# Hybrid encoder layer on one core: the first transfers of the SP queue in another order, and two waits and four small operations moved later

## The chip, the core and the metric

The kernel runs on one core of a Trainium2 chip. The metric is device time in microseconds of one execution. Each engine (TensorE, VectorE, ScalarE, GpSimd) works through its own list of instructions in order and waits on semaphores; SyncE (SP) issues nearly all DMA transfers from one list, in the order in which they are written.

## The reference, cut to what matters

Two inputs, 256 and 512 tokens of 1024 features, go through one encoder layer. Cut to its start:

```
def encoder_layer(x, norm1, w_in, ...):
    u = rmsnorm(x, norm1)
    z = u @ w_in                      # 1024 -> 384 + 256 + 32 + 512 + 512 columns
    q_lat, kv_lat, k_rope, x_br, g_br = jnp.split(z, [c1, c2, c3, c4], axis=-1)
    att = mla(q_lat, kv_lat, k_rope, q_norm, w_q_up, kv_norm, w_kv_up)
    lru = rglru_mixer(x_br, g_br, conv_w, conv_b, w_rg, b_rg, w_ig, b_ig, lru_lambda)
    ...
def rglru_direction(x, w_r, b_r, w_i, b_i, lam, reverse):
    ...
    log_a = -LRU_C * r * jax.nn.softplus(-lam.astype(jnp.float32))
```

Behind it come the output projection with the residual, a second norm, a mixture of 32 experts of which each token takes two, and a final norm.

## The kernel before

The 768 tokens are six x tiles of 128 rows. The change lies in the first 45 us, in the input stage. For each x tile, ScalarE squares and sums the row (`row_norm`, L1041) and takes the root with eps from the constants (L1045); VectorE takes the reciprocal (L1503) and writes x times rstd times the norm row (L1506, tile `un`); TensorE turns the tile with eight transposes against the identity in the constants (L660); ScalarE writes a rounded copy `u_high` (`input_high`, L1051) and VectorE the rest `u_low` (`input_low`, L1514). The columns of `w_in` come in 14 tiles of 1024 x 128 (the one for the rotary key is narrower): of each, ScalarE (the first four, `weight_high`, L1057) or GpSimd writes `w_high`, and GpSimd writes `w_low` (L535). TensorE multiplies in three passes, high by high, low by high, high by low, 24 matmuls to a unit (L716). Units 0 to 3 are the first four w_in tiles on the 256 tokens of the first input (x tiles 0 and 1); from unit 4 on come units of 512 columns too, which need all six x tiles. TensorE's order is: turn x tiles 0 and 1; unit 0; turn x tile 2; unit 1; turn tile 3; unit 2; turn tile 4; unit 3; turn tile 5; unit 4 and on. ScalarE moves finished units from PSUM to SBUF (`move_out`, L1079); the first goes into `xb`, which GpSimd clears at the start (semaphore `pads`, L524).

`cols` holds gains, biases and the decay parameters lambda by partition, `consts` the identity, eps and tables, `norm_row` the first norm's gain in all partitions. VectorE begins with four small operations on `cols` (L1496 to L1499) that prepare the decay constants; they are needed only behind the input stage.

The order is written out by hand for every engine. In SP's list a load of w_in tile t waits, from t = 2 on, until `w_low` of tile t - 2 is written (L366), and what stands behind it waits too.

Of the kernel before, what the change touches and what calls it, by code (L numbers as in the profile page):

```python
# [4 lines left out]
P = 128  # L5
TOK, PROMPT = 768, 256
NT = TOK // P
D = 1024
# [27 lines left out]
COLS = {}  # L36
# [16 lines left out]
def encoder_layer(nc, A_x, A_cols, A_consts, A_rope, A_rows, A_win, A_wq, A_wkv, A_wrg, A_wig, A_wout,  # L53
                  A_wrt, A_wgate, A_wup, A_wdown, y_prompt, y_sample):
    f32, f32r, i32 = mybir.dt.float32, mybir.dt.float32r, mybir.dt.int32
    ALU = mybir.AluOpType
# [3 lines left out]
    with ctx:  # L60
        def sb(name, shape, dt=f32):
            return ctx.enter_context(nc.sbuf_tensor(name, shape, dt))
# [32 lines left out]
        consts = sb("consts", [P, NCONSTS])  # L95
        cols = sb("cols", [P, NCOLS])
        norm_row = sb("norm_row", [P, D])
# [29 lines left out]
        def col(name, j, p0=0, p1=P):  # L127
            a = COLS[name] + j
            return cols[p0:p1, a:a + 1]
# [47 lines left out]
        lam_t = small[:, 32:80].rearrange("p (k n) -> p k n", k=6)  # L177
        hb_r = small[:, 80:88]
        hb_i = small[:, 88:96]
# [100 lines left out]
        def g(name):  # L280
            return S[name]
# [10 lines left out]
        def width(kind):  # L292
            return RP if kind == "k" else P
# [57 lines left out]
        def _(sp):  # L351
            xv = A_x.rearrange("(i p) d -> i p d", p=P)

            def load_x(i):
                if i == 5:
                    sp.wait_ge(g("un"), 1)
                sp.dma_start(xin[i], xv[i]).then_inc(s_xin[i], 16)
            wv = A_win.rearrange("(c p) n -> p c n", p=P)

            def load_w(t):  # L360

                kind, c = w_tiles[t]
                if t >= 2:
                    sp.wait_ge(g("wlo"), t - 1)
                col0, m = first_col[kind] + c * P, width(kind)
                sp.dma_start(w_raw[:, t % 2, :, 0:m], wv[:, :, col0:col0 + m]).then_inc(g(f"wr{t % 2}"), 16)  # L366
            load_x(0)
            sp.dma_start(cols[:], A_cols).then_inc(g("cols"), 16)
            sp.dma_start(consts[:], A_consts).then_inc(g("consts"), 16)
            sp.dma_start(norm_row[:], A_rows[3:4, 0:D].to_broadcast([P, D])).then_inc(g("n1"), 16)  # L370
            load_w(0)
            load_x(1)
            load_w(1)
            load_x(2)
            load_w(2)
            load_x(3)
            load_w(3)
# [650 lines left out]
        def _(ac):  # L1028
            chain = [0]

            def link(ins):
                chain[0] += 1
                ins.then_inc(g("ach"), 1)
                ac.wait_ge(g("ach"), chain[0])
# [4 lines left out]
            def row_norm(i):  # L1039
                ac.wait_ge(s_xin[i], 16)  # L1040
                link(ac.activation(junk, xin[i], ACT.Square, accum_out=ssq[:, i:i + 1]))  # L1041
                if i == 0:
                    ac.wait_ge(g("consts"), 16)
                    ac.wait_ge(g("cols"), 16)
                ac.activation(rstd1[:, i:i + 1], ssq[:, i:i + 1], ACT.Sqrt, bias=eps, scale=1.0 / D).then_inc(g("sd"), 1)  # L1045

            def input_high(i):

                for j in range(2):
                    ac.wait_ge(g("uTp"), 2 * i + j + 1)  # L1050
                    ac.activation(uh[:, 4 * j:4 * j + 4, i * P:(i + 1) * P],  # L1051
                                  psum[4 + 2 * (i % 2) + j][:, :].rearrange("p (c t) -> p c t", c=4),
                                  ACT.Copy).then_inc(g("uTh"), 1)

            def weight_high(t):
                ac.wait_ge(g(f"wr{t % 2}"), 16 * (t // 2 + 1))
                ac.activation(wh[:, t, :, :], w_raw[:, t % 2, :, :], ACT.Copy).then_inc(g("whi"), 1)  # L1057

            def move_out(u):

                kind, c, n = units[u]
                ac.wait_ge(g("zp"), u + 1)
                t0, tn = CHUNKS[n]
                if kind == "x":
                    dst = xb[:, c, XOFF[n] + 1:XOFF[n] + 1 + tn]
                elif kind == "z":
                    dst = zl[:, c, t0:t0 + tn]
                elif kind == "k":
                    dst = kr[0:RP, t0:t0 + tn]
                else:  # L1070
                    dst = gg[:, c, t0:t0 + tn]
                if kind == "z":
                    ins = ac.activation(sqz[:, c, t0:t0 + tn], psum[u % ZB][:, 0:tn], ACT.Square)
                    if n == 1:
                        ins.then_inc(g("sqz"), 1)
                    gain = col("q_norm", c) if c < QC else col("kv_norm", c - QC)
                    ac.activation(dst, psum[u % ZB][:, 0:tn], ACT.Copy, scale=gain).then_inc(g("ze"), 1)
                else:
                    ac.activation(dst, psum[u % ZB][0:width(kind), 0:tn], ACT.Copy).then_inc(g("ze"), 1)  # L1079

            ac.wait_ge(g("pads"), 1)
            row_norm(0)
            row_norm(1)
            weight_high(0)
            input_high(0)
            input_high(1)
            weight_high(1)
            row_norm(2)
            for i in range(2, NT):
                if i + 1 < NT:  # L1090
                    row_norm(i + 1)
                input_high(i)
                if i < W_RING:
                    weight_high(i)
                move_out(i - 2)

            ac.wait_ge(g("lam"), 1)
# [386 lines left out]
        def _(v):  # L1484
            chain = [0]

            def link(ins):
                chain[0] += 1
                ins.then_inc(g("dch"), 1)
                v.wait_ge(g("dch"), chain[0])  # L1490
            v.memset(ahead, 1.0).then_inc(g("ahead"), 1)
            v.wait_ge(g("cols"), 16)


            lam = cols[:, COLS["lam"]:COLS["lam"] + 8]
            link(v.tensor_scalar(lam_t[:, 4, :], lam, -1.0, None, ALU.mult))  # L1496
            link(v.tensor_tensor(lam_t[:, 0, :], lam_t[:, 4, :], lam, ALU.max))
            link(v.tensor_scalar(hb_r, cols[:, COLS["b_rg"]:COLS["b_rg"] + 8], 0.5, None, ALU.mult))
            v.tensor_scalar(hb_i, cols[:, COLS["b_ig"]:COLS["b_ig"] + 8], 0.5, None, ALU.mult).then_inc(g("lam"), 1)  # L1499
            def norm_rows(i):  # L1500

                v.wait_ge(g("sd"), i + 1)
                link(v.reciprocal(rstd1[:, i:i + 1], rstd1[:, i:i + 1]))  # L1503
                if i >= 2:
                    v.wait_ge(g("uTp"), 2 * (i - 1))
                v.scalar_tensor_tensor(out=un[:, i % 2, :], in0=xin[i], scalar=rstd1[:, i:i + 1], in1=norm_row[:],  # L1506
                                       op0=ALU.mult, op1=ALU.mult).then_inc(g("un"), 1)

            def input_low(i):

                for j in range(2):
                    cut = (slice(None), slice(4 * j, 4 * j + 4), slice(i * P, (i + 1) * P))
                    v.wait_ge(g("uTh"), 2 * i + j + 1)
                    v.tensor_tensor(ul[cut], psum[4 + 2 * (i % 2) + j][:, :].rearrange("p (c t) -> p c t", c=4),  # L1514
                                    uh[cut].bitcast(f32), ALU.subtract).then_inc(g("uT"), 1)
# [3 lines left out]
            input_low(0)  # L1519
            input_low(1)  # L1520
            norm_rows(2)
            for i in range(2, NT):
                if i + 1 < NT:
                    norm_rows(i + 1)
                input_low(i)
# [379 lines left out]
```

## Time and profile before

| | |
|---|---|
| median of 3 runs | 727.15 us |
| the 3 runs | 723.83 to 727.35 us |
| the profiled execution | 726.99 us, span 725.1 us |
| TensorE busy, share of the span | 669.6 us, 92% |
| VectorE, ScalarE, GpSimd busy | 400.3, 265.6, 190.3 us |
| mean granted clock of TensorE | 0.971 |

The span reaches from the first to the last instruction of the profile; the time of the execution has a little more around it. Busy times are sums over the span and don't tell which engine is waited for at a given place; for that the chain of work that ended last and the engines' timelines are read.

### The profile page before, as it was taken

What the parts mean: (1) busy time and instruction counts of PE and PEld (TensorE: products, weight loads), DVE (VectorE), ACT (ScalarE), POOL (GpSimd) and SP (SyncE); (2) the same over time, 40 slices, a digit from 0 to 9 for tenths busy, and PEclk for the clock granted to TensorE, in tenths of its full rate; (3) what the DMA queues carried; (4) which work ended last, traced back from release to release, by engine and by line L of the source; (5) the groups of instructions that cost most, each with busy time, mean ns of one, the idle gap of its engine ahead of it and who ended that gap; (6) DMA issues with size and microseconds to landing.
All of it is one profiled execution on the core that took longest, in us unless ns stands there. A gap on an engine that the chain in (4) does not pass through costs nothing.

```text
span 725.1 us, 11900 instructions
## 1 busy us (share of the span) xinstructions
PE 669.6 (92%) x4204; PEld 462.0 (64%) x4204; DVE 400.3 (55%) x945; ACT 265.6 (37%) x498; POOL 190.3 (26%) x181
## 2 busy tenths in 40 slices
PE   2999999999999999999998478999999999997985
PEld 1978887886548777788887445565555555454531
DVE  3663589544976667648888585763223232322317
ACT  4634787733666767831122001111111111111123
POOL 4344354102911582200000101321222323222110
PEclk9999999999999999999998589999999999999998
DMA  6912211020070000034225999999999999999367
GB/s 193 273 43 66 59 30 30 19 105 30 0 266 24 1 1 1 19 135 139 88 98 175 400 397 416 357 411 412 417 416 414 416 418 417 417 416 403 145 237 294
DMA packets 50911, 155.83 MB, mean 215 GB/s; under 512 B 9508, under 2 KB 22948, under 8 KB 42672
## 3 DMA queue, kind: packets, MB, share of 16 engines
q1 hardware_dynamic: 42704, 136.32, 48.7%
q0 software_dynamic: 6432, 12.60, 4.6%
q10 hardware_dynamic: 1728, 6.29, 2.3%
q8 instruction: 28, 0.46, 0.3%
q14 instruction: 19, 0.16, 0.1%
HBM read 169.86 MB, written 19.92 MB: 262 GB/s over the span
## 4 chain that ended last, share of the span: by engine, by line
PE 71%; SPq 9%; DMA 7%; DVE 7%; issue 2%; ACT 2%; POOL 0%; POOLq 0%; DVEq 0%; ACTq 0%
PE bank L716 16%; PE bank L959 9%; PE bank L876 8%; PE bank L984 6%; PE bank L754 5%; SPq L466 5%; PE bank L773 4%; DMA ring<-in_w_up 4%; PE bank L737 3%; SPq L474 3%; PE bank L763 2%; PE bank L933 2%; PE bank L671 2%; PE bank L839 2%; PE bank L741 1%
## 5 line engine op out<-in xcount | busy, mean ns | idle before, releaser
L959 PE MATMUL bank<-ring,tmp 128*64 128x256 f32 x896 | 103.5, 390 | 5.9 <-DMA ring<-in_w_up 5.0
L959 PEld LDWEIGHTS bank<-ring,tmp 128*64 128x64 f32 x896 | 66.8, 141 | 44.5 <-issue 13.9
L607 POOL DMA_INDIRECT expert_rows<-mix,row_now x40 | 40.0, 999 | 194.4 <-ACT mix L1272 170.8
L716 PE MATMUL bank<-u_high,w_high 128*128 128x256 f32 (+3 forms) x224 | 78.3, 350 | 3.4 <-DVE u_low L1514 3.0
L716 PE MATMUL bank<-u_low,w_high 128*128 128x256 f32 (+3 forms) x224 | 76.4, 341 | 0.0
L716 PE MATMUL bank<-u_high,w_low 128*128 128x256 f32 (+3 forms) x224 | 76.4, 341 | 0.0
L1265 ACT ACTIVATE rope<-bank 64x256 f32<-64x256 f32 x40 | 15.1, 378 | 155.2 <-PE bank L959 140.2
L1777 DVE SCALAR_TENSOR_TENSOR rope<-rope,bank 64x256 f32<-64x256 f32 x40 | 16.6, 414 | 79.7 <-ACT rope L1265 78.9
L1272 ACT ACTIVATE mix<-bank,gate_now 128x512 f32<-128x512 f32 x40 | 27.5, 687 | 89.6 <-PE bank L984 89.6
L597 POOL DMA_INDIRECT tmp<-xn_rows,idx_now x22 | 23.3, 1059 | 124.8 <-DVE idx_now L1370 107.5
L984 PE MATMUL bank<-ring,rope 128*64 128x512 f32 x224 | 55.2, 614 | 0.0
L876 PE MATMUL bank<-ring_parts,mix_parts 128*128 128x512 f32 x180 | 50.2, 393 | 0.0
L716 PEld LDWEIGHTS bank<-u_high,w_high 128*128 128x128 f32 (+1 forms) x224 | 42.2, 188 | 9.4 <-DVE u_low L1514 3.6
L1787 DVE COPY rope<-bank 128x128 f32<-128x128 f32 x40 | 11.7, 292 | 62.7 <-PE bank L970 62.7
L716 PEld LDWEIGHTS bank<-u_low,w_high 128*128 128x128 f32 (+1 forms) x224 | 42.3, 189 | 5.3
L716 PEld LDWEIGHTS bank<-u_high,w_low 128*128 128x128 f32 (+1 forms) x224 | 42.3, 189 | 5.2
L754 PE MATMUL bank<-ring 96*128 96x512 f32 (+1 forms) x96 | 44.6, 548 | 0.3 <-ACT ring L1157 0.3
L959 PE MATMUL bank<-mix,tmp 128*64 128x256 f32 x384 | 42.5, 379 | 0.0
L773 PE MATMUL bank<-ring,softm 128*128 128x64 f32 x320 | 41.3, 268 | 0.0
L535 POOL TENSOR_TENSOR w_low<-ring,w_high 128x1024 fp32r<-128x1024 f32 (+1 forms) x14 | 35.3, 2520 | 18.8 <-ACT w_high L1057 18.0
L773 PEld LDWEIGHTS bank<-ring,softm 128*128 128x128 f32 x320 | 39.4, 191 | 0.9 <-issue 0.9
L1657 DVE TENSOR_REDUCE small<-bank 128x1 f32<-128x512 f32 (+1 forms) x48 | 28.9, 601 | 18.9 <-PE bank L754 17.3
(288 smaller groups left out, 1226.8 us busy)
## 6 DMA issues: line engine op xcount, KB each, us to landing
ring<-in_w_up SPq DMA_DIRECT2D x28, 1024.0 KB, 19.9
ring<-in_w_down SPq DMA_DIRECT2D x28, 1024.0 KB
ring<-in_w_gate SPq DMA_DIRECT2D x28, 1024.0 KB, 17.0
mix<-in_w_gate SPq DMA_DIRECT2D x12, 1024.0 KB, 11.2
mix<-in_w_up SPq DMA_DIRECT2D x12, 1024.0 KB, 14.3
mix<-in_w_down SPq DMA_DIRECT2D x12, 1024.0 KB, 17.1
ring<-in_w_in SPq DMA_DIRECT2D x13, 512.0 KB, 4.0
ring<-expert_rows SPq DMA_DIRECT2D x12, 512.0 KB, 8.5
```

The lines of the kernel that those rows point to most:

```text
L466: sp.dma_start(w[:, part * DC * F:(part + 1) * DC * F], view[bass.ds(code & (NE - 1), 1)].rearrange("e p n -> (e p) n"), bounds_check="ski ...
L535: po.tensor_tensor(wl[:, k, :, 0:m], raw, wh[:, k, :, 0:m].bitcast(f32), ALU.subtract).then_inc(g("wlo"), 1)
L597: po.indirect_dma_start(xg[:, k, :], None, xn_d, bass.IndirectOffsetOnAxis(idx_now[:, k:k + 1], 0), bounds_check=TOK - 1, oob_is_err=False ...
L607: po.indirect_dma_start(ys_d.rearrange("r (t n) -> (r t) n", t=2), bass.IndirectOffsetOnAxis(row_now[:, 2 * j + q:2 * j + q + 1], 0), ysb[ ...
L716: last = pe.matmul(psum[u % ZB][0:m, 0:tn], w[:, t % W_RING, k, 0:m], x[:, k, t0:t0 + tn], start=(k == 0 and p == 0), stop=(k == DC - 1 an ...
L754: pe.matmul(psum[n % 3][:, 0:kn], qT[0:96, h, i * P:(i + 1) * P], kT[0:96, h, k0:k0 + kn], start=True, stop=True).then_inc(g("sc"), 1)
L773: last = pe.matmul(psum[5][:, 0:VH], probT[:, n % 2, b * P:(b + 1) * P], V[:, k0 // P + b, h * VH:(h + 1) * VH], start=(b == 0), stop=(b = ...
L876: last = pe.matmul(psum[2 + 2 * half + k][:, :], x, w[:, out], start=(c == 0 and p == 0), stop=(c == LC - 1 and p == 2))
L959: last = pe.matmul(psum[q][t * WB:(t + 1) * WB, 0:F], xT[:, j, c, q * WB:(q + 1) * WB], w[:, (t * DC + c) * F:(t * DC + c + 1) * F], start ...
L984: last = pe.matmul(psum[4 + q][t * WB:(t + 1) * WB, :], hT[:, f, :], w[:, f * D + t * 512:f * D + (t + 1) * 512], start=(f == 0), stop=(f ...
L1272: ac.activation(ysb[:, q, :], psum[4 + q][:, :], ACT.Copy, scale=gate_now[:, 2 * j + q:2 * j + q + 1]).then_inc(g("ye"), 1)
L1657: link(v.tensor_reduce(mx[:, k:k + 1], psum[n % 3][:, 0:kn], AX.X, ALU.max))
```

## The change

On SP the norm row, the constants and x tile 1 now stand behind x tile 0; the first two w_in tiles come behind x tiles 1 and 2, and `cols` comes last of this batch, ahead of w_in tile 2. ScalarE no longer waits for the cleared `xb` ahead of everything, nor for `cols` ahead of its first root; it waits for both ahead of its first `move_out`. VectorE's four decay operations, with their wait for `cols`, stand behind the third `norm_rows`.

```
@@ block.sync
             load_x(0)
+            sp.dma_start(norm_row[:], A_rows[3:4, 0:D].to_broadcast([P, D])).then_inc(g("n1"), 16)
+            sp.dma_start(consts[:], A_consts).then_inc(g("consts"), 16)
+            load_x(1)
+            load_w(0)
+            load_x(2)
+            load_w(1)
             sp.dma_start(cols[:], A_cols).then_inc(g("cols"), 16)
-            sp.dma_start(consts[:], A_consts).then_inc(g("consts"), 16)
-            sp.dma_start(norm_row[:], A_rows[3:4, 0:D].to_broadcast([P, D])).then_inc(g("n1"), 16)
-            load_w(0)
-            load_x(1)
-            load_w(1)
-            load_x(2)
             load_w(2)
             load_x(3)
             load_w(3)
@@ block.scalar
                 if i == 0:
                     ac.wait_ge(g("consts"), 16)
-                    ac.wait_ge(g("cols"), 16)
...
-            ac.wait_ge(g("pads"), 1)
             row_norm(0)
             row_norm(1)
             weight_high(0)
...
                 if i < W_RING:
                     weight_high(i)
+                if i == 2:
+                    ac.wait_ge(g("pads"), 1)
+                    ac.wait_ge(g("cols"), 16)
                 move_out(i - 2)
@@ block.vector
             v.memset(ahead, 1.0).then_inc(g("ahead"), 1)
-            v.wait_ge(g("cols"), 16)
-            lam = cols[:, COLS["lam"]:COLS["lam"] + 8]
-            link(v.tensor_scalar(lam_t[:, 4, :], lam, -1.0, None, ALU.mult))
...
...
             norm_rows(2)
+            v.wait_ge(g("cols"), 16)
+            lam = cols[:, COLS["lam"]:COLS["lam"] + 8]
+            link(v.tensor_scalar(lam_t[:, 4, :], lam, -1.0, None, ALU.mult))
+            link(v.tensor_tensor(lam_t[:, 0, :], lam_t[:, 4, :], lam, ALU.max))
+            link(v.tensor_scalar(hb_r, cols[:, COLS["b_rg"]:COLS["b_rg"] + 8], 0.5, None, ALU.mult))
+            v.tensor_scalar(hb_i, cols[:, COLS["b_ig"]:COLS["b_ig"] + 8], 0.5, None, ALU.mult).then_inc(g("lam"), 1)
             for i in range(2, NT):
```

SP's list at its start, before. `tmp` and `softm` receive x tiles, `ring` the w_in tiles, each row is one transfer:

```order
L357 DMA tmp<-in_x 128x1024
L368 DMA cols<-in_cols 128x65
L369 DMA consts<-in_consts 128x626
L370 DMA norm_row<-in_rows 128x1024
L366 DMA ring<-in_w_in 128x8x128
L357 DMA tmp<-in_x 128x1024
L366 DMA ring<-in_w_in 128x8x128
L357 DMA tmp<-in_x 128x1024
```

And the same place now:

```order
L357 DMA tmp<-in_x 128x1024
L368 DMA norm_row<-in_rows 128x1024
L369 DMA consts<-in_consts 128x626
L357 DMA tmp<-in_x 128x1024
L366 DMA ring<-in_w_in 128x8x128
L357 DMA tmp<-in_x 128x1024
L366 DMA ring<-in_w_in 128x8x128
L374 DMA cols<-in_cols 128x65
```

The second x tile moved ahead of the first w_in tile, and the columns behind both w_in tiles.

VectorE's list at its start, before; `small` holds the small vectors:

```order
L1491 MEMSET small 128x1
L1496 TENSOR_SCALAR small<-cols 128x8
L1497 TENSOR_TENSOR small<-small,cols 128x8
L1498 TENSOR_SCALAR small<-cols 128x8
L1499 TENSOR_SCALAR small<-cols 128x8
L1503 RECIPROCAL small<-small 128x1
L1506 SCALAR_TENSOR_TENSOR tmp<-tmp,small,norm_row 128x1024
```

Now, from the u_low parts of x tiles 0 and 1 to the norm of x tile 3 (the line numbers are those of the changed kernel):

```order
L1507 TENSOR_TENSOR u_low<-bank,u_high 128x4x128 x4
L1496 RECIPROCAL small<-small 128x1
L1499 SCALAR_TENSOR_TENSOR tmp<-tmp,small,norm_row 128x1024
L1519 TENSOR_SCALAR small<-cols 128x8
L1520 TENSOR_TENSOR small<-small,cols 128x8
L1521 TENSOR_SCALAR small<-cols 128x8
L1522 TENSOR_SCALAR small<-cols 128x8
L1496 RECIPROCAL small<-small 128x1
L1499 SCALAR_TENSOR_TENSOR tmp<-softm,small,norm_row 128x1024
```

The four operations on `cols` moved from ahead of all norms to between those of x tiles 2 and 3.

## Rows read from the trace of the kernel before

**Rows 1.** The head of each answer: the core and its span.

```profile
core 0 of [0], span 725.1 us
```

**Rows 2.** Chain that ended last, in order of time: start us, us, what.

```profile
3.04 8.85 DMA tmp<-in_x
...
14.97 1.98 PE bank L660 x8
...
18.35 5.49 PE bank L716 x24
...
24.67 1.08 ACT u_high L1051 x2
...
29.27 3.14 PE bank L716 x24
...
38.64 24.93 PE bank L716 x120
```

**Rows 3.** Timeline of SP's queue: start us, us, line, transfer.

```profile
2.09 0.43 SPq L370 DMA_DIRECT2D norm_row<-in_rows x1
2.57 0.43 SPq L366 DMA_DIRECT2D ring<-in_w_in x1
...
4.54 4.39 SPq L357 DMA_DIRECT2D tmp<-in_x x1
...
17.58 0.58 SPq L357 DMA_DIRECT2D softm<-in_x x1
```

**Rows 4.** DMA issues of those moments: KB, us from issue to landing.

```profile
norm_row<-in_rows SPq DMA_DIRECT2D x1, 512.0 KB, 6.7
ring<-in_w_in SPq DMA_DIRECT2D x1, 512.0 KB, 8.0
...
cols<-in_cols SPq DMA_DIRECT2D x1, 32.5 KB, 3.2
...
tmp<-in_x SPq DMA_DIRECT2D x1, 512.0 KB, 10.2
...
softm<-in_x SPq DMA_DIRECT2D x1, 512.0 KB, 4.8
```

**Rows 5.** Timeline of ScalarE: start, us, instruction, idle before and releaser.

```profile
5.17 1.06 ACT L1041 ACTIVATE tmp<-tmp 128x1024 f32<-128x1024 f32 x1 [2.95 <-POOL xb L524]
...
13.30 1.04 ACT L1057 ACTIVATE w_high<-ring 128x1024 fp32r<-128x1024 f32 x1
...
16.97 0.60 ACT L1051 ACTIVATE u_high<-bank 128x512 fp32r<-128x512 f32 x1 [0.26 <-PE bank L660]
...
22.42 1.06 ACT L1041 ACTIVATE tmp<-softm 128x1024 f32<-128x1024 f32 x1 [2.54 <-DMA softm<-in_x]
```

**Rows 6.** Timeline of VectorE, and one row of GpSimd.

```profile
4.33 0.83 DVE L1496 TENSOR_SCALAR small<-cols 128x8 f32<-128x8 f32 x1 [3.48 <-DMA cols<-in_cols]
...
5.60 0.17 DVE L1499 TENSOR_SCALAR small<-cols 128x8 f32<-128x8 f32 x1
8.85 0.16 DVE L1503 RECIPROCAL small<-small 128x1 f32<-128x1 f32 x1 [3.08 <-DMA norm_row<-in_rows]
...
14.43 2.71 POOL L535 TENSOR_TENSOR w_low<-ring,w_high 128x1024 fp32r<-128x1024 f32 x1 [9.29 <-ACT w_high L1057]
...
20.11 2.01 DVE L1506 SCALAR_TENSOR_TENSOR tmp<-tmp,small,norm_row 128x1024 f32<-128x1024 f32 x1
...
23.92 0.16 DVE L1503 RECIPROCAL small<-small 128x1 f32<-128x1 f32 x1 [1.81 <-ACT small L1045]
```

**Rows 7.** Windows: busy us (instructions) by engine, granted clock, DMA share, GB/s.

```profile
4.00:5.00 1.00, 0.00 (x0) 0.00 (x0) 0.67 (x1) 0.00 (x0) 1.00 (x1) 1.00 1.06 195
18.35:23.60 5.25, 5.25 (x24) 5.25 (x25) 2.17 (x2) 2.65 (x7) 2.37 (x1) 1.00 0.91 250
38.60:167.50 128.90, 128.86 (x664) 104.34 (x664) 77.82 (x82) 73.87 (x111) 43.22 (x23) 1.00 0.16 48
400.00:430.00 30.00, 18.64 (x176) 14.79 (x176) 21.05 (x97) 0.70 (x3) 3.14 (x3) 0.60 0.97 396
```

More of the change, by code:

```diff
@@ L1491, in _ @@
             v.memset(ahead, 1.0).then_inc(g("ahead"), 1)
-            v.wait_ge(g("cols"), 16)
-            lam = cols[:, COLS["lam"]:COLS["lam"] + 8]
-            link(v.tensor_scalar(lam_t[:, 4, :], lam, -1.0, None, ALU.mult))
-            link(v.tensor_tensor(lam_t[:, 0, :], lam_t[:, 4, :], lam, ALU.max))
-            link(v.tensor_scalar(hb_r, cols[:, COLS["b_rg"]:COLS["b_rg"] + 8], 0.5, None, ALU.mult))
-            v.tensor_scalar(hb_i, cols[:, COLS["b_ig"]:COLS["b_ig"] + 8], 0.5, None, ALU.mult).then_inc(g("lam"), 1)
             def norm_rows(i):
```

## Prediction

> **What bounds the kernel now.** I read the chain of work that ended last, in order of time, to see what the start of the program waits for; then the SP queue and the landings of its transfers, since the chain begins with one; then the timelines of ScalarE, VectorE and GpSimd, to see what is ready early and what late; and last the windows, for how far a change at the start is carried. The chain leaves the queue at one row: the second x tile, issued at 3.04, lands 8.85 us later, at 11.89 [rows 2]. From there to the first projection matmul at 18.35 runs a fixed series of 6.46 us: square, root, reciprocal, scaled row, eight transposes, u_high, u_low. Unit 0, its 24 matmuls, takes 5.49 us; unit 2, as large, takes 3.14 [rows 2]. That is 256 columns in about 0.22 and 0.12 us, TensorE at 1.2 and then at 2.4 GHz, though the granted clock is shown as 1.00 [rows 7]. Behind it the front alternates: turned x tile, u_high, w_high, w_low on GpSimd, and unit 2 starts at 29.27 when w_low is there. From 38.64 on TensorE stands almost nowhere: it is busy 128.86 of 128.90 us [rows 7]. A gain that reaches 38.64 is therefore carried to 167.5, and whatever waits later is released by engines, so the queue moves along.
>
> The profiled execution took 726.99 us with a span of 725.1 [rows 1]; it lies 0.16 below the median of the three runs, 727.15, so a saving read from it may be taken from the median.
>
> **What is removed from before the second x tile.** Landing times are issue time plus time to landing. The norm row lands at 2.09 + 6.7 = 8.8, the first w_in tile at 2.57 + 8.0 = 10.6, the second x tile at 11.9 [rows 2 to 4]. Landings follow the order of issue here, spaced by the bytes in between. Now the w_in tile (512 KB) and the columns (32.5 KB) stand behind x tile 1. The w_in tile's step is 10.6 - 8.8 = 1.8 us. The columns have no step to themselves in the rows; at 195 GB/s, the rate while such transfers ran [rows 7], 33 kB are 0.17 us. Together 1.95: x tile 1 would land at about 9.95. Low end: the same 512 KB, when x tile 1 itself moved it, took 11.9 - 10.6 = 1.3 us, and the columns nothing, so 1.3. High end: 524 kB at 195 GB/s are 2.7, with the columns 2.9. I take 1.95, because it is the step of the very transfer that is moved.
>
> The Trainium skill, in DMA: Bandwidth & Descriptors, section Anatomy of one DMA, fits a transfer as about 2.0 us fixed plus bytes over 436 GB/s. By it the w_in tile would cost only 1.2 us of queue and the columns 0.08, and the saving would be 1.3 instead of 1.95; the step of 1.8 us in this trace disagrees, and the sum goes by the trace.
>
> **Tile 0.** Its square waited 2.95 us for the clearing of xb on GpSimd and starts at 5.17; without that wait it starts when its data is there. This gives nothing: VectorE's reciprocal at 8.85 waits for the norm row, not for ScalarE [rows 5, 6]. The norm row and the constants change places but both still precede x tile 1. Both are in by about 8.8 - 0.17 = 8.6; if the constants are last, ScalarE's root comes in between (1.5 less the square's 1.06, 0.4 us), so the reciprocal stands within 0.2 us of 8.85. From the reciprocal on its steps are those of tile 1, whose transposes end at 14.97 + 1.98 = 16.95, 3.55 us after its reciprocal at about 11.89 + 1.5 = 13.4 (1.5 is what lies between square and reciprocal, 22.42 and 23.92 [rows 5, 6]). So tile 0 is turned by 8.85 + 0.2 + 3.55 = 12.6, before tile 1's transposes would begin at 9.95 + (14.97 - 11.89) = 13.0 [rows 2]. No cost, by 0.4 us.
>
> **What is now late instead: the first w_in tile.** It lands after the same bytes as x tile 1 did, without the columns: 11.89 - 0.17 = 11.7. ScalarE's conversion (1.04) and GpSimd's w_low (2.71) [rows 5, 6] with some 0.15 of handing over end at 15.6. Tile 1's path ends at 9.95 + 6.46 = 16.4. The cover is 0.8 us, and it is also the cap: TensorE can't start before 15.6, so the gain at this place is at most 18.35 - 15.65 = 2.7 even if x tile 1 lands at 9.0. On ScalarE, which converts before it evacuates, the conversion and two u_high (1.04 + 1.08) end at 13.8, against the second tile's first u_high at 14.1: 0.3 us of cover.
>
> **The later transfers.** The third x tile landed last of the first batch, 4.54 + 10.2 = 14.7 [rows 3, 4]; so in the new order the second w_in tile and the columns are in by then. ScalarE converts the second w_in tile after its last early u_high, 16.97 + 0.60 before [rows 5], 15.6 now: covered by 0.9. The third w_in tile and the fourth x tile wait in SP for w_low of the first, which ends at 15.6 instead of 14.43 + 2.71 = 17.14, so they leave 1.55 earlier. The fourth x tile landed at 17.58 + 4.8 = 22.4 and ScalarE had waited 2.54 us for it [rows 3 to 5]; now 20.85. Its square and root (1.5 us) end at 22.35; behind them stands the evacuation of the third turned tile, 24.67 before [rows 2], 22.7 if moved by 1.95. Cover 0.35. This is a second cap: that evacuation can't move by more than 2.3.
>
> **The moved operations and waits.** The four decay operations last from 4.33 to 5.77, 1.44 us, and lay in the wait for the norm row. Now they stand between the third and the fourth normalised row, where VectorE is idle from 20.11 + 2.01 = 22.12 to 23.92, 1.80 us [rows 6]. They fit, with 0.3 us to spare; if the cover were gone, what they hold up is the reciprocal at 23.92, then the fourth row, some 1.3 us after it, which TensorE turns only after unit 1, in the microsecond or two before unit 2 at 29.27: a further 2 us of cover. ScalarE's wait for the clearing and the columns now stands before the first move_out, after 24.67 in time, with data there by 14.7. Queued behind it are the fifth square, and through it the fifth tile, but it can't bind. Cost of both: zero.
>
> **Sum.** Only one term lies on the path: 1.95 us at the first matmul. With unit 0 at the same low level the whole chain, 18.35, 24.67, 29.27, 38.64 [rows 2], moves by the same 1.95. 727.15 - 1.95 = 725.2.
>
> **Rivals.**
> The saving is hidden. Another arrival takes the place of x tile 1: the transfers of both norm row and constants are the slow ones, or w_in tile 0 lands late. For it: only 195 GB/s flowed at 4 to 5 us [rows 7], and the covers of 0.3 and 0.4 us are thin. Against: steps of 1.8 and 1.3 are in the rows with the same neighbours. If the w_in tile lands at 13.5, it ends at 17.4 and the gain is 0.9; at 14.4 it is zero. Time 726.3 to 727.2. Chance 0.15.
>
> More than the sum. At the start 2.3 and 2.7 are the caps. Part comes if TensorE rises to 2.4 GHz within unit 0: 24 x 0.1 = 2.3 us are lost to the low level there, but the fourth x tile lets through only 0.35 of it. A saving of more than 3.6 needs the late stage too. It would come in the stage at 400 to 430, where the granted clock is 0.60 and VectorE and DMA set the pace [rows 7]. Time 721.5 to 723.5. Chance 0.17.
>
> Slower. The place is the stage of output projection and routing: TensorE's clock falls there earlier than now, because the first matmuls and everything behind them stand elsewhere in time. Granted 0.60 over 30 us in 400 to 430 is a mean of both levels, some 24 us at the lower. Each microsecond at the lower level in a matmul-bound stretch costs about half a microsecond. It decides from 4 us on (the 1.95 is gone), and 11 us would make it slower by over 0.5%: 731. Nothing in the change causes it. Chance 0.06.
>
> **How the numbers follow.** Forecast (1.3 to 2.9 saved, capped at 2.7: 724.5 to 725.9): 0.62; hidden 0.15; more 0.17; slower 0.06. What this kernel's measurement can tell is about 0.5%, 3.6 us; the three runs span 3.5. So forecast and hidden are both within it, more is the only case beyond below: faster 0.17, same 0.77, slower 0.06. The range takes in hidden and most of more, and for the runs' own spread a little above the old median: 722.0 to 728.2.
>
> **What the new profile would show.** Right: the second x tile lands near 10 (9.0 to 10.6), ScalarE's first square starts before 5.17 and its second square near 10; the first 256-column matmul stands at 16.4 and waits for u_low, not for w_low; unit 4, the first of 512 columns, at 36.7; decay operations near 20 to 22 in VectorE's idle time, first move_out without a wait for columns; the long stretch again without gaps. Wrong: that matmul waits for w_low of GpSimd (the w_in tile is late); ScalarE's first root waits for the constants beyond 9; the square of the fourth x tile delays u_high after unit 0; or 38.64 becomes 36.7 and the end does not follow, which would put the difference into the clock at 370 to 430.

## The result, and the profile after

The changed kernel takes 723.69 us (median of 15 runs, 720.5 to 725.7) against 725.46 us for the kernel before (15 runs of the same session). The ratio on record for these runs is 0.9951, with a 95% interval of 0.9935 to 0.9966: 3.6 us less, between 2.5 and 4.7. It is not the quotient of the two medians: these lie 1.8 us apart, the means of the 15 runs 2.7. A second timing of the changed kernel gave 0.9960 (0.9937 to 0.9983), 2.9 us, with 3.3 us between the medians and 3.1 between the means. The saving forecast was 1.95 us, below the first interval and in the lower part of the second (1.2 to 4.6 us). Both intervals are clear of no change; how far the saving is above the forecast the times alone tell only roughly, since the runs of one kernel lie 5 to 6 us apart. The profiles tell it better for the start. The profiled execution took 723.69 us with a span of 721.9.

The chain of waits of the changed kernel, at its start (start us, us, what):

```profile
2.57 7.90 DMA ring<-in_w_in
...
10.49 1.07 ACT w_high L1056
...
11.63 2.36 POOL w_low L535
...
14.43 5.43 DMA softm<-in_x
...
21.27 1.07 ACT u_high L1050 x2
...
25.83 4.50 PE bank L716 x24
...
31.36 2.88 PE bank L716 x24
...
36.68 8.46 PE bank L716 x36
```

It no longer begins with x tile 1, as [rows 2] did, but with the first w_in tile; through w_low it releases x tile 3 (`softm`), which lands at 19.86. Unit 2 (the row of 4.50 us) starts at 25.83, 3.44 us ahead of the 29.27 before, and then takes 1.36 us longer. Unit 4 starts at 36.68, ahead by 1.96.

What SP issued, from its timeline, and the time from issue to landing:

```profile
1.15 0.42 SPq L368 DMA_DIRECT2D norm_row<-in_rows x1
1.63 0.42 SPq L369 DMA_DIRECT2D consts<-in_consts x1
2.09 0.43 SPq L357 DMA_DIRECT2D tmp<-in_x x1
2.57 0.47 SPq L366 DMA_DIRECT2D ring<-in_w_in x1
```

```profile
norm_row<-in_rows SPq DMA_DIRECT2D x1, 512.0 KB, 5.2
consts<-in_consts SPq DMA_DIRECT2D x1, 313.0 KB, 5.6
tmp<-in_x SPq DMA_DIRECT2D x1, 512.0 KB, 6.6
ring<-in_w_in SPq DMA_DIRECT2D x1, 512.0 KB, 7.9
```

Sums of issue and landing: norm row 6.3, constants 7.2, x tile 1 8.7, first w_in tile 10.5. Before, the norm row was in at 8.8 and x tile 1 at 11.9 [rows 3, 4]. So x tile 1 is 3.2 us early, not 1.95, and norm row and constants are both in 1.6 us before they were.

ScalarE, VectorE, GpSimd and TensorE at the places of [rows 5, 6]:

```profile
4.03 1.06 ACT L1041 ACTIVATE tmp<-tmp 128x1024 f32<-128x1024 f32 x1 [1.82 <-DMA tmp<-in_x]
...
7.35 0.29 ACT L1044 ACTIVATE small<-small,consts 128x1 f32<-128x1 f32 x1 [2.17 <-DMA consts<-in_consts]
8.71 1.06 ACT L1041 ACTIVATE tmp<-tmp 128x1024 f32<-128x1024 f32 x1 [1.07 <-DMA tmp<-in_x]
...
19.89 1.06 ACT L1041 ACTIVATE tmp<-softm 128x1024 f32<-128x1024 f32 x1 [3.29 <-DMA softm<-in_x]
```

```profile
7.75 0.16 DVE L1496 RECIPROCAL small<-small 128x1 f32<-128x1 f32 x1 [6.90 <-ACT small L1044]
...
16.83 2.04 DVE L1499 SCALAR_TENSOR_TENSOR tmp<-tmp,small,norm_row 128x1024 f32<-128x1024 f32 x1
18.80 0.16 DVE L1519 TENSOR_SCALAR small<-cols 128x8 f32<-128x8 f32 x1
...
19.40 0.17 DVE L1522 TENSOR_SCALAR small<-cols 128x8 f32<-128x8 f32 x1
21.40 0.16 DVE L1496 RECIPROCAL small<-small 128x1 f32<-128x1 f32 x1 [1.83 <-ACT small L1044]
```

```profile
11.63 2.35 POOL L535 TENSOR_TENSOR w_low<-ring,w_high 128x1024 fp32r<-128x1024 f32 x1 [6.50 <-ACT w_high L1056]
```

```profile
15.07 0.39 PE L716 MATMUL bank<-u_high,w_high 128*128 128x256 f32 x1 [1.41 <-DVE u_low L1507]
15.29 0.28 PE L716 MATMUL bank<-u_high,w_low 128*128 128x256 f32 x1
15.41 0.28 PE L716 MATMUL bank<-u_low,w_high 128*128 128x256 f32 x1
...
25.83 0.39 PE L716 MATMUL bank<-u_high,w_high 128*128 128x256 f32 x1 [1.80 <-POOL w_low L535]
...
26.89 0.28 PE L716 MATMUL bank<-u_low,w_high 128*128 128x256 f32 x1
27.01 0.33 PE L716 MATMUL bank<-u_high,w_high 128*128 128x256 f32 x1
27.14 0.41 PE L716 MATMUL bank<-u_high,w_low 128*128 128x256 f32 x1
27.35 0.42 PE L716 MATMUL bank<-u_low,w_high 128*128 128x256 f32 x1
```

Four things can be read from these rows. ScalarE's first square now waits for its data alone, and VectorE's first reciprocal now waits for ScalarE's root, which waits for the constants. The four decay operations take 0.77 us (18.80 to 19.57) in VectorE's idle time, and the reciprocal behind them still waits 1.83 us for ScalarE. TensorE runs unit 0 at 2.4 GHz from its start (matmuls 0.12 us apart, the unit in 3.14 us against 5.49 before), and this gains nothing for unit 2: that one waits for the w_low which comes by way of x tile 3, now for 1.80 us. And TensorE falls back within unit 2: its starts go from 0.12 us apart to 0.21 (2.4 GHz, then 1.2), until unit 2 ends. This fall gives back 1.4 us of the 3.4. A window over it, with the granted clock third from the end; the same window of the third profile of this kernel stands in the section on the experiments, under "The clock":

```profile
25.00:30.00 5.00, 4.17 (x24) 4.17 (x25) 4.48 (x6) 3.45 (x7) 3.16 (x2) 0.71 0.73 203
```

### The profile page after: what moved, and what is told of

The parts are those of the page before. It is cut to its first block, busy times and chain, and to the rows that moved or that the text cites. A ratio compares the mean times of both kernels' runs of the same rounds, so it can differ in the third digit from the quotient of the medians.

```text
span 721.9 us, 11900 instructions
## 1 busy us (share of the span) xinstructions
PE 666.9 (92%) x4204; PEld 459.5 (64%) x4204; DVE 399.6 (55%) x945; ACT 265.6 (37%) x498; POOL 190.9 (26%) x181
## 4 chain that ended last, share of the span: by engine, by line
PE 70%; SPq 10%; DMA 8%; DVE 7%; issue 2%; ACT 2%; POOL 1%; POOLq 0%; DVEq 0%; ACTq 0%
PE bank L716 16%; PE bank L959 9%; PE bank L876 8%; PE bank L984 6%; SPq L466 6%; PE bank L754 5%; PE bank L773 4%; DMA ring<-in_w_up 4%; PE bank L737 3%; SPq L474 3%; PE bank L763 2%; PE bank L933 2%; PE bank L671 2%; PE bank L839 2%; PE bank L741 1%
## 5 line engine op out<-in xcount | busy, mean ns | idle before, releaser
L959 PE MATMUL bank<-ring,tmp 128*64 128x256 f32 x896 | 102.3, 387 | 5.9 <-DMA ring<-in_w_up 5.0
L959 PEld LDWEIGHTS bank<-ring,tmp 128*64 128x64 f32 x896 | 66.2, 140 | 43.9 <-issue 13.2
L984 PE MATMUL bank<-ring,rope 128*64 128x512 f32 x224 | 55.1, 614 | 0.0
L1788 DVE COPY rope<-bank 128x128 f32<-128x128 f32 x40 | 11.7, 292 | 60.5 <-PE bank L970 60.5
L959 PE MATMUL bank<-mix,tmp 128*64 128x256 f32 x384 | 42.5, 379 | 0.0
L1658 DVE TENSOR_REDUCE small<-bank 128x1 f32<-128x512 f32 (+1 forms) x48 | 28.9, 602 | 19.1 <-PE bank L754 17.5
```

What stands on the lines that cost most here:

```text
L959: last = pe.matmul(psum[q][t * WB:(t + 1) * WB, 0:F], xT[:, j, c, q * WB:(q + 1) * WB], w[:, (t * DC + c) * F:(t * DC + c + 1) * F], start ...
L984: last = pe.matmul(psum[4 + q][t * WB:(t + 1) * WB, :], hT[:, f, :], w[:, f * D + t * 512:f * D + (t + 1) * 512], start=(f == 0), stop=(f ...
L1658: link(v.tensor_reduce(mx[:, k:k + 1], psum[n % 3][:, 0:kn], AX.X, ALU.max))
```

## The experiments

All runs below are whole kernels with the reference's computation. "Unit 4" is the first matmul of 512 columns, from where TensorE runs on without gaps ([rows 7]); a gain that is there at unit 4 is carried to the output projection, whose first long stretch starts 270.42 us behind unit 4 in all five profiles of the two kernels. The landing of a transfer is its issue plus the time to landing. Apart from the two kernels compared, each arrangement was profiled once. How far one list of transfers varies by itself can be read where it was run more than once: the old list landed x tile 1 at 11.9, 12.4 and 11.7 (the kernel before twice, waits and operations alone), the new one at 8.6 to 8.9 (five profiles). Steps of 0.2 or 0.3 us are within that. The summary; the last column is the ratio to the kernel before with its interval, where timed:

| kernel | norm row, constants in by | x tile 1 lands | first 256-column matmul | unit 4 | ratio |
|---|---|---|---|---|---|
| before, profiles 1 and 2 | 8.8; 9.3 | 11.9; 12.4 | 18.35; 18.91 | 38.64; 38.71 | 1 |
| waits and operations alone | 8.4 | 11.7 | 18.18 | 38.38 | 1.000 (0.998 to 1.002) |
| ... and columns last | 8.1 | 11.5 | 17.89 | 38.03 | 1.000 (0.997 to 1.003) |
| ... and norm row ahead of constants (w_in second) | 7.1 | 10.4 | 16.84 | 36.62 | 0.9971 (0.9944 to 0.9999) |
| changed kernel, profiles 1 to 3 | 7.2; 7.3; 7.3 | 8.7; 8.9; 8.6 | 15.07; 15.30; 14.94 | 36.68; 35.03; 35.09 | 0.9951 and 0.9960 |
| changed, constants first | 8.5 | 9.9 | 16.33 | 36.38 | 0.9972 (0.9951 to 0.9993) |
| changed, columns second | 9.1 | 10.5 | 16.81 | 36.73 | 0.9969 (0.9938 to 0.9999) |
| order alone, waits as before | 7.4 | 8.8 | 21.05 | 40.91 | 1.0038 (1.0014 to 1.0061) |
| x tiles 3 and 4 early | 7.2 | 8.6 | 15.03 | 34.34 | 0.9951 (0.9925 to 0.9977) |
| ... and norm row stored 128 times | 6.7 | 8.1 | 14.36 | 32.90 | 0.9938 (0.9915 to 0.9960) |

**Waits and operations alone.** SP's first transfers in the old order, the rest as in the changed kernel, against which the edit is shown:

```
             load_x(0)
+            sp.dma_start(cols[:], A_cols)...
+            sp.dma_start(consts[:], A_consts)...
             sp.dma_start(norm_row[:], ...)...
-            sp.dma_start(consts[:], A_consts)...
-            load_x(1)
             load_w(0)
-            load_x(2)
+            load_x(1)
             load_w(1)
-            sp.dma_start(cols[:], A_cols)...
+            load_x(2)
             load_w(2)
```

> The transfers stand in the old order; only the waits on the clearing and on the columns and the four decay operations are where the changed kernel has them. Theory (all of the gain is the order of transfers): the second x tile still lands at about 11.9, tile 0's reciprocal still waits for the norm row until about 8.8, the first 256-column matmul stays near 18.35 and the time within 0.5 us of before. Rival (the waits held something back): the first matmul comes 1 us or more earlier and the time falls by 1 to 3.5 us.

VectorE's first reciprocal still waits for the norm row:

```profile
8.37 0.16 DVE L1496 RECIPROCAL small<-small 128x1 f32<-128x1 f32 x1 [7.53 <-DMA norm_row<-in_rows]
```

The rival (1 us or more earlier) is out: first matmul at 18.18, ratio 1.000. The moved waits and operations give nothing by themselves.

**Order alone.** The other half, new order of transfers in the kernel before:

> Only the transfers stand in the new order; ScalarE still waits for the columns ahead of its first root and VectorE begins with the four decay operations. Theory (the moved waits are what lets the new order work, since the columns now land last of the batch): the root of tile 0 and VectorE's first operation start only at about 13.7, when the columns are in; tile 0's row ends at about 15.6, its transposes at 17.6, tile 1's at 19.5, the first 256-column matmul stands near 21, unit 4 near 41, and the time is 2 to 3.5 us above before. Rival (the moved waits are of no matter): the first matmul near 15.1 as in the changed kernel.

```profile
13.66 0.17 DVE L1496 TENSOR_SCALAR small<-cols 128x8 f32<-128x8 f32 x1 [12.81 <-DMA cols<-in_cols]
```

```profile
13.74 0.29 ACT L1045 ACTIVATE small<-small,consts 128x1 f32<-128x1 f32 x1 [7.43 <-DMA cols<-in_cols]
```

Both engines wait for the columns, the last of the batch. Unit 4 begins at 40.91, 2.2 to 2.3 us behind before, and the ratio is 1.0038, 2.8 us slower. x tile 1 landed at 8.8 as in the changed kernel and was of no use. So the two halves only work together.

**Columns last.** As the run with waits and operations alone, and the columns behind x tile 2:

> The old order of transfers with the columns alone moved to the end of the first batch (and the waits as in the changed kernel). Theory 1: x tile 1 lands near 11.7, the first matmul near 18.1, time 0.2 us below before. Theory 2: x tile 1 lands near 10.7, the first matmul near 17.2, time about 1 us below before.

```profile
tmp<-in_x SPq DMA_DIRECT2D x1, 512.0 KB, 8.9
```

Issued at 2.57: x tile 1 at 11.5, 0.2 us earlier than with the columns second, and no 1.2 as by theory 2. Theory 1 and the prediction's 0.17 us fit in this order, though so small a step is within what the old list varies by.

**The w_in tile.** The changed kernel with the first w_in tile ahead of x tile 1 again:

```
-            load_x(1)
             load_w(0)
+            load_x(1)
             load_x(2)
```

> As the changed kernel, but the first w_in tile stands ahead of x tile 1 again. Theory 1: x tile 1 lands 3 us later than in the changed kernel, near 11.7, and 2.5 to 3.5 us of the gain are gone. Theory 2: it lands 1.8 us later, the w_in tile's own step, near 10.5; the first matmul stands near 17.0 and about 1.5 to 2 us are gone.

```profile
consts<-in_consts SPq DMA_DIRECT2D x1, 313.0 KB, 5.5
ring<-in_w_in SPq DMA_DIRECT2D x1, 512.0 KB, 7.0
tmp<-in_x SPq DMA_DIRECT2D x1, 512.0 KB, 7.8
```

Issued at 1.62, 2.09 and 2.57: x tile 1 at 10.4, against 8.7. The w_in tile is worth 1.7 us, as by theory 2. Up to x tile 1 this list differs from that of the run before it only in that the norm row leaves ahead of the constants, and x tile 1 lands 1.1 us earlier. That was the missing part, and I tested it apart.

**Constants first.** The changed kernel with those two in their old order:

```
             load_x(0)
+            sp.dma_start(consts[:], A_consts)...
             sp.dma_start(norm_row[:], ...)...
-            sp.dma_start(consts[:], A_consts)...
             load_x(1)
```

> As the changed kernel, but the constants leave before the norm row, as they did before the change. Theory (the order of these two is worth what the old order lost, 1.1 us between the runs with the w_in tile second and with the columns last): x tile 1 lands near 9.8 instead of 8.7 and the first 256-column matmul stands near 16.2. Rival (those two runs differed by chance): x tile 1 lands near 8.7. Time: 0 to 1 us above the changed kernel's.

```profile
norm_row<-in_rows SPq DMA_DIRECT2D x1, 512.0 KB, 6.9
tmp<-in_x SPq DMA_DIRECT2D x1, 512.0 KB, 7.8
```

Issued at 1.63 and 2.09: 8.5 and 9.9. The constants were in at 4.8, but the norm row behind them took 3.7 us more; in the changed kernel the norm row takes 2.3 behind x tile 0 and the constants 0.9. The swap is worth 1.2 us at x tile 1 (1.0 to 1.3 against the three profiles of the changed kernel), so the 1.1 us between the two runs before was no chance.

**Columns second.** The changed kernel with the columns directly behind x tile 0:

> As the changed kernel, but the columns stay second in the queue. Theory 1 (the first w_in tile alone held up the second x tile by about 3 us, the columns are worth 0.2): x tile 1 lands near 8.9 instead of 8.7 and the time is the changed kernel's within 0.3 us. Theory 2 (the narrow rows of the columns near the start cost about 1.2 us of everything behind them): x tile 1 lands near 9.8, the constants near 8.2, the first matmul near 16.2, and about 1 us of the gain is lost.

The norm row landed at 8.1, the constants at 9.1, x tile 1 at 10.5, 1.8 us later than in the changed kernel. Theory 2 had the direction and was still too small: the same 32.5 KB cost 0.2 us with the constants behind them and 1.8 with the norm row behind them. In these profiles the price of a small transfer depends on what follows it; why, no run shows. The time, 0.9969, can't be told from the changed kernel's.

**Why the swap counts.** Three kernels with the constants first, each executed once: the norm row read from 128 stored copies in place of one row read 128 times, the rows of constants filled up to 2560 bytes, and both. The first two edits:

```
-            sp.dma_start(norm_row[:], A_rows[3:4, 0:D].to_broadcast([P, D])).then_inc(g("n1"), 16)
+            sp.dma_start(norm_row[:], A_norm).then_inc(g("n1"), 16)
...
-NCONSTS = _at
+NCONSTS = _at + 14
```

> As the run with the constants first, but the norm row is read from 128 stored copies of it (one row of memory per partition) and not 128 times from one row. Theory A (many reads of one row of memory are slow, and slower behind the constants): both are in by about 7.0, the norm row's step is 1.3 us like an x tile's, and x tile 1 lands at 8.3 or earlier. Theory B (the slow stretch at 3 to 6 us belongs to the odd row lengths of the constants, or to the start of the queue): the norm row's step stays at 2.5 us or more and x tile 1 lands near 9.8.

> As the run with the constants first, with each partition's row of constants filled up with 14 zeros, from 2504 to 2560 bytes. Theory (rows of odd length disturb what is moved behind them): the norm row's step behind the constants falls from 3.7 to about 2.3 us and x tile 1 lands near 8.7. Rival (it is the place in the queue and not the row's length): norm row at 8.5, x tile 1 at 9.9 as there.

> Constants first, with rows filled up to 2560 bytes, and the norm row from stored copies, both at once. If the two together make up what the order costs, the norm row lands by 7.3 and x tile 1 near 8.7. If the place in the queue costs by itself, the norm row lands near 7.8 and x tile 1 near 9.2.

The norm row landed at 7.9, 8.2 and 8.0, x tile 1 at 9.3, 9.7 and 9.4, beside 8.5 and 9.9 without an edit. The repeated read costs some 0.6 us at x tile 1 (0.3 with the rows filled up); the 0.2 for the odd rows is within what one list varies by. With both gone 0.7 us of the distance to 8.7 remain (0.5 to 0.8 against the three profiles), so neither is the whole cause. What remains goes with the place in the queue; why, these runs don't show.

**The clock.** The changed kernel twice more, and the kernel before once more:

> The changed kernel once more. Theory (the profiled execution of it was one in which TensorE fell to 1.2 GHz within unit 2, and others keep the level): landings within 0.2 us of the first profile, x tile 1 near 8.7, first 256-column matmul near 15.1, but unit 2 in 3.1 us instead of 4.5 and unit 4 near 35.3, so that the whole saving at unit 4 is 3.3 us and not 1.96. Rival (the fall belongs to this order, since TensorE waits 1.80 us ahead of unit 2): the same fall again and unit 4 near 36.7.

> The changed kernel a third time: x tile 1 between 8.6 and 9.0, first 256-column matmul between 15.0 and 15.4. If the fall to 1.2 GHz in unit 2 is rare, unit 4 stands near 35.0 as in the second profile; if it is common with this order, near 36.7 as in the first.

> The kernel before once more, to see how far one execution's landings are those of others: x tile 1 within 0.3 us of 11.9, the first 256-column matmul within 0.3 of 18.35, unit 4 between 37.5 and 38.7 by the moment at which TensorE rises to 2.4 GHz.

The third profile of the changed kernel:

```profile
25.22 0.39 PE L716 MATMUL bank<-u_high,w_high 128*128 128x256 f32 x1 [1.60 <-POOL w_low L535]
...
29.50 0.39 PE L716 MATMUL bank<-u_high,w_high 128*128 128x256 f32 x1 [0.26 <-POOL w_low L535]
...
35.09 0.50 PE L716 MATMUL bank<-u_high,w_high 128*128 128x512 f32 x1 [1.57 <-DVE u_low L1507]
```

```profile
25.00:30.00 5.00, 4.52 (x36) 4.28 (x37) 4.03 (x6) 4.68 (x10) 2.56 (x2) 1.00 0.80 215
```

TensorE waits 1.60 us ahead of unit 2, nearly as long as in the first profile, and keeps 2.4 GHz: the granted clock is 1.00 here and 0.71 there. The second profile had no fall either (unit 4 at 35.03); there the rise came only within unit 0, at 19.1, and TensorE waited 0.55 us ahead of unit 2. So in this kernel the wait of 1.6 to 1.8 us came with the executions in which unit 0 runs at 2.4 GHz (3.14 us in the first and third profile, 4.87 in the second), and the fall came in one of these two. Whether unit 0 is fast or slow makes no difference at unit 4: 35.09 and 35.03. Against 38.64 and 38.71 the saving at unit 4 is 3.6 us in two of three profiles and 2.0 in one.

What is saved at unit 4 is not what is saved at the end. The starts in each profile, with "experts" for the first 64 matmuls of an expert's first products (L959):

| profile | unit 4 | output projection | experts | span |
|---|---|---|---|---|
| before, 1 | 38.64 | 309.06 | 456.08 | 725.1 |
| before, 2 | 38.71 | 309.13 | 456.31 | 723.8 |
| changed, 1 | 36.68 | 307.10 | 454.26 | 721.9 |
| changed, 2 | 35.03 | 305.45 | 452.87 | 720.5 |
| changed, 3 | 35.09 | 305.51 | 454.43 | 721.6 |

The third profile loses 1.7 us between the output projection and the experts, in one group of eight matmuls of an expert's second product (L984), beside the same group of the first (start us, us, what):

```profile
446.82 3.54 PE bank L984 x8
```

```profile
448.33 1.87 PE bank L984 x8
```

In the window from 445 to 452 the granted clock is 0.76 there and 1.00 in the first profile. The kernel before has such a fall too, in its first profile and not in its second:

```profile
668.21 5.36 PE bank L959 x32
```

```profile
668.62 3.67 PE bank L959 x32
```

The first profile of the changed kernel did not have this one (3.67 us for the same group), and its span, 721.9, lies 3.2 us below the 725.1 of the first profile before, though it was only 1.96 us ahead at unit 4. One such fall is as large as what a step at the start is worth. The means of the spans lie 3.1 us apart, near the two timings of 3.6 and 2.9 us.

**The next late transfer.** x tiles 3 and 4 with the first batch:

```
             sp.dma_start(cols[:], A_cols)...
+            load_x(3)
+            load_x(4)
             load_w(2)
-            load_x(3)
             load_w(3)
-            load_x(4)
             load_x(5)
```

> As the changed kernel, but x tiles 3 and 4 leave with the first batch, ahead of w_in tile 2 and its wait. Theory (the profile of the changed kernel names the fourth x tile, x tile 3, as the next late thing: its square at 19.89 holds back u_high, w_high and w_low, and unit 2 waits 1.80 us): the square of x tile 3 comes at about 16.6, unit 2 begins near 24.0 instead of 25.83, TensorE keeps 2.4 GHz through unit 2, unit 4 begins near 34 to 34.8 instead of 36.68, and the time is 1 to 2 us below the changed kernel's. Rival (something else of the same age is next, or TensorE's clock takes the gain back): unit 4 within 0.5 us of the changed kernel's.

```profile
16.47 1.04 ACT L1041 ACTIVATE tmp<-softm 128x1024 f32<-128x1024 f32 x1
```

```profile
24.99 0.39 PE L716 MATMUL bank<-u_high,w_high 128*128 128x256 f32 x1 [0.47 <-POOL w_low L535]
...
34.34 0.50 PE L716 MATMUL bank<-u_high,w_high 128*128 128x512 f32 x1 [1.57 <-DVE u_low L1507]
```

The square of x tile 3 comes at 16.47 instead of 19.89, and the wait ahead of unit 2 falls to 0.47 us. Unit 4 is 0.7 us ahead of the two better profiles of the changed kernel, in one profile. The time doesn't tell them apart: 0.9951 beside 0.9960 in the same session. In the profile the gain is not kept either: the experts start at 453.53, between the 452.87 and 454.43 of those two.

**With the norm row stored as well.**

> The version with x tiles 3 and 4 in the first batch, and the norm row read from 128 stored copies. Theory (the repeated read of one row of memory costs a little wherever it stands): x tile 1 lands 0.4 to 0.6 us earlier than in the changed kernel, near 8.2, first 256-column matmul near 14.6, unit 4 near 34, time 0 to 1 us below that version's. Rival (directly behind x tile 0 the repeated read is already fast): landings as there, 8.6.

x tile 1 at 8.1, the first 256-column matmul at 14.36, at 2.4 GHz from its start; unit 4 at 32.90, which is 5.7 us ahead of before. The experts start at 453.83, where 2.3 to 2.5 us of that are left. The ratio is 0.9938 (0.9915 to 0.9960), 4.5 us less than before: the lowest measured, but its interval overlaps that of the changed kernel, so the time doesn't show it to be faster than that one.

## Why the prediction was wrong in size

**The step that failed** is the sum at "What is removed from before the second x tile", through a sentence of "Tile 0": "The norm row and the constants change places but both still precede x tile 1. Both are in by about 8.8 - 0.17 = 8.6". Behind it is the premise "Landings follow the order of issue here, spaced by the bytes in between". I priced transfers by the bytes ahead and took the order of two that both stand ahead as worth nothing. They were in by 7.2. The landings of the old list already spoke against the premise: by this row, issued at 1.62, the constants were in at 6.9.

```profile
consts<-in_consts SPq DMA_DIRECT2D x1, 313.0 KB, 5.3
```

So 313 KB took 2.6 us behind the columns (in at 4.3), and the norm row, 512 KB, 1.9 behind them; in the new list the norm row takes 2.3 and the constants 0.9. The landing of x tile 1 came out as 8.7 in place of 9.95, and the runs give it as terms, from one list to the next: columns 11.7 to 11.5, 0.2 us (0.17 forecast); norm row ahead of constants 11.5 to 10.4, 1.1 us (nothing forecast); w_in tile 10.4 to 8.7, 1.7 us (1.8 forecast). Together 3.0, measured from 11.7; the two profiles of the kernel before had 11.9 and 12.4, so it is 3.2 us from the first to the first. The 2.9 us that I gave as a high end comes near, but for another reason, 195 GB/s for the w_in tile. That the order is the term is shown by the swap; why it costs is open.

**The caps fell with it.** The first w_in tile was to land at 11.7 and allow no more than 2.7 us at the first matmul. Standing behind the same two transfers, it landed at 10.5, and GpSimd's w_low took 2.35 instead of 2.71 us; w_low was ready at 13.98, ahead of u_low, and the matmul began 3.28 us early. The second cap, x tile 3, was right in kind: its square is on the new chain, with 3.29 us of waiting. It left with w_low at 14.43 instead of 16.0, so that 2.3 us became 3.4 at the evacuation behind it (24.67 to 21.27). The run with the early x tiles puts what it still cost at 0.7 us at unit 4.

**What held.** From landing to first matmul 6.37 us (6.46 forecast). The decay operations cost nothing and neither do ScalarE's moved waits; the run with waits alone shows that they give nothing either, and the run with the order alone that they are needed. Nothing was lost between unit 4 and the output projection: the long stretch of 60 matmuls there starts 1.96 us early in the first profile (307.10 after 309.06), as much as at unit 4. The times at the end follow less closely, as the table under "The clock" shows.

**TensorE's clock.** The forecast of unit 4, 36.7, was met by the first profile (36.68), by two errors that cancel: 1.3 us more at the landing, 1.4 us lost to a fall to 1.2 GHz in unit 2. The premise of the sum, unit 0 "at the same low level", held in none of the three profiles to the unit's end: it took 3.14, 4.87 and 3.14 us against 5.49. Had I counted that as gain I would have been wrong too; the cap by x tile 3, named under the rivals, let nothing of it through to unit 4. What I had not followed is where that time goes: into the wait ahead of unit 2, 0.45 us before and 1.80 in the first profile, and behind that wait the clock fell. I had looked for loss only in the late stage. One of three profiles had this fall.

**The chances.** "More than the sum", 0.17, comes nearest to what happened; its mechanism is not what the runs show: the rise in unit 0 gave nothing, and 3.6 us are there at unit 4 in two profiles, without the late stage. In the first pair of profiles the late stage has its share, by a fall that the kernel before had in one of two profiles; that is luck. With the caps taken as hard I left hardly any chance to a saving between 2.7 and 3.6. The measured 723.69 us lies in the range, by the range's width and by luck: the median of before was 725.46 there and not 727.15, and the saving is 3.6 us by the ratio, not 1.95. The fit of the Trainium skill in DMA: Bandwidth & Descriptors, Anatomy of one DMA, gave 1.2 us, an estimate, for the 512 KB of the w_in tile; taking it away gave 1.7 here. The section states the fit for single transfers that GpSimd issues, and these are SP's with others in flight, so the difference doesn't contradict it.

## What to carry to other kernels

Where a kernel begins with a batch of transfers, the landing of the one that is waited for depends on the order of all that stand ahead of it, not only on their bytes: read from the landings what each took behind its own neighbour, and give a permutation ahead of it a range of its own, here 1.0 to 1.3 us for 825 KB. Moving a transfer back needs the waits on it moved back too, or it costs more than it saves. And when a chain is shortened, look for the next arrival by the same chain (here x tile 3), and at whether TensorE now has a longer wait, behind which its clock fell in one of three profiles here. A gain at the start can be read from one profile to some 0.3 to 0.7 us; at the end single falls of the clock, 1.4 to 1.7 us each here, hide it, and they come in the kernel before as in the changed one.

## What was not expected of the hardware

- 32.5 KB in rows of 260 bytes directly behind x tile 0 cost 0.2 us when the constants followed and 1.8 us when the norm row did (x tile 1 at 11.5 and 11.7; at 8.7 and 10.5).
- Norm row then constants were in 3.2 us behind x tile 0, constants then norm row 4.4 us (7.2 after 4.0; 8.5 after 4.1). With the constants first, stored copies in place of one row read 128 times brought the norm row in 0.6 us earlier (8.5 to 7.9); padding the constants' rows to 2560 bytes 0.3 (8.5 to 8.2), no more than one list varies by.
- With the same program and nearly the same waits (1.80 and 1.60 us), TensorE fell to 1.2 GHz within a unit of 24 matmuls in one execution and not in another. The granted clock of the windows shows this fall (0.71), but not the low level at the start: in [rows 7] it reads 1.00 over the 5.25 us in which 24 matmuls of 256 columns went by at 1.2 GHz. The spacing of the matmuls has to be read beside it.
